# Delta heads' triangular inverses: the level of width 32 on packed 32x32 blocks, and two turns as products with the unit block

## The reference, cut to what matters

```
Gamma = jnp.exp(jnp.where(incl, G[..., :, None] - G[..., None, :], -jnp.inf))
kb = kc * bc[..., None]
A = jnp.where(strict, jnp.einsum('nbhcd,nbhsd->nbhcs', kb, kc) * Gamma, 0.0)
Tinv = lax.linalg.triangular_solve(eye + A, jnp.broadcast_to(eye, A.shape), left_side=True,
                                   lower=True, unit_diagonal=True)
u = jnp.einsum('nbhcs,nbhse->nbhce', Tinv, vc * bc[..., None])
w = jnp.einsum('nbhcs,nbhsd->nbhcd', Tinv, kb * jnp.exp(G)[..., None])
```

## Time and profile before

| | us |
|---|---|
| median of 3 runs | 2392.61 |
| lowest and highest run | 2390.42, 2393.23 |
| span of the profiled execution | 2388.0 |
| TensorE busy in it | 2303.5 (96%) |
| VectorE busy | 1345.3 (56%) |
| ScalarE busy | 580.2 (24%) |
| GpSimd busy | 185.4 (8%) |

### The profile page before, as it was taken

The page is one execution under the profiler, slowest core; times in us unless marked ns, Lnnn a source line. Parts: engine busy times, 40 slices in busy tenths (PEclk is TensorE's granted clock), DMA queues, the critical chain, the costliest instruction groups (busy, mean ns, idle before and its releaser), DMA issues.

```text
span 2388.0 us, 35106 instructions
## 1 busy us (share of the span) xinstructions
PE 2303.5 (96%) x13789; PEld 1951.4 (82%) x13789; DVE 1345.3 (56%) x2163; ACT 580.2 (24%) x1483; POOL 185.4 (8%) x252
## 2 busy tenths in 40 slices
PE   6999999999998999899999999999999999989998
PEld 3788889964546888788888999888899968668997
DVE  4377748564544777346776585677646521545521
ACT  3111111222222444441111113211111211442210
POOL 1100000001111333000000000000000000000000
PEclk7999999999999999999999999999999999999999
DMA  8555548532210000123555575355455523023562
GB/s 290 203 159 176 177 114 237 133 96 74 67 57 32 1 1 1 37 71 107 176 175 165 140 214 152 97 173 176 142 137 149 165 71 106 18 71 124 176 181 66
DMA packets 311468, 293.11 MB, mean 123 GB/s; under 512 B 6713, under 2 KB 292019, under 8 KB 311219
## 3 DMA queue, kind: packets, MB, share of 16 engines
q1 hardware_dynamic: 290611, 215.90, 30.5%
q0 software_dynamic: 20736, 75.51, 10.1%
HBM read 290.34 MB, written 1.05 MB: 122 GB/s over the span
## 4 chain that ended last, share of the span: by engine, by line
PE 89%; DVE 4%; ACT 3%; issue 1%; DMA 1%; SPq 0%; POOL 0%; DVEq 0%; POOLq 0%; ACTq 0%
PE bank L810 39%; PE bank L932 17%; PE bank L664 13%; PE bank L1010 3%; PE bank L774 2%; PE bank L1308 2%; PE bank L1130 2%; PE bank L1141 1%; PE bank L1069 1%; DMA mring<-in_w_mod 1%; PE bank L642 1%; DVE room L2374 1%; PE bank L1100 1%; PE bank L1151 1%; ACT hs L1726 1%
## 5 line engine op out<-in xcount | busy, mean ns | idle before, releaser
L810 PE MATMUL bank<-hs,ring 128*128 128x256 f32 (+1 forms) x2112 | 446.8, 356 | 5.6 <-ACT hs L1480 4.8
L810 PEld LDWEIGHTS bank<-hs,ring 128*128 128x128 f32 x2112 | 366.2, 192 | 54.6 <-issue 11.0
L932 PE MATMUL bank<-big,ring 128*128 128x128 f32 x2904 | 330.1, 275 | 0.0
L932 PEld LDWEIGHTS bank<-big,ring 128*128 128x128 f32 x2904 | 327.4, 192 | 0.2
L810 PE MATMUL bank<-room,big 128*128 128x256 f32 (+1 forms) x1408 | 296.1, 353 | 0.0
L810 PEld LDWEIGHTS bank<-room,big 128*128 128x128 f32 x1408 | 242.4, 191 | 26.6
L1928 DVE SCALAR_TENSOR_TENSOR mring<-mring,cond 128x1024 f32<-128x1024 f32 x196 | 240.4, 1279 | 9.9 <-DMA mring<-in_w_mod 9.9
L664 PE MATMUL bank<-hs,ring 128*128 128x512 f32 (+2 forms) x592 | 233.4, 548 | 0.0
L664 PEld LDWEIGHTS bank<-hs,ring 128*128 128x128 f32 (+1 forms) x592 | 109.8, 188 | 105.9 <-issue 102.2
L544 POOL DMA_DIRECT2D mring<-in_w_mod x144 | 76.2, 529 | 1074.0 <-DVE mring L1922 487.4
L810 PE MATMUL bank<-room,ring 128*128 128x256 f32 (+1 forms) x704 | 149.3, 355 | 2.5 <-ACT room L1516 1.8
(11 more groups left out here) (317 smaller groups left out, 3171.7 us busy)
## 6 DMA issues: line engine op xcount, KB each, us to landing
ring<-in_ffn_w_in SPq DMA_DIRECT2D x88, 1024.0 KB, 5.7
ring<-in_ffn_w_out SPq DMA_DIRECT2D x56, 1408.0 KB, 7.3
mring<-in_w_mod POOLq DMA_DIRECT2D x144, 512.0 KB, 4.1
ring<-in_gdn_w_in SPq DMA_DIRECT2D x16, 1024.0 KB, 5.7
ring<-in_diff_w_in SPq DMA_DIRECT2D x12, 1024.0 KB, 5.1
ring<-in_gdn_w_out SPq DMA_DIRECT2D x4, 1024.0 KB, 4.9
ring<-in_diff_w_out SPq DMA_DIRECT2D x4, 1024.0 KB, 4.9
cst<-in_consts SPq DMA_DIRECT2D x1, 1344.0 KB, 10.0
```

Of the source, the lines that this page charges most:

```text
L810: last = mm(bank[:, (g0 + b) % 4, 0:width], w[:, k, jj * P:(jj + 1) * P], rhs[:, k, 0:width], start=start and k == 0, stop=(k == KC // 2 - ...
L932: last = mm(bank[:, (go + b) % 4, 0:P], w[:, k, :], rhs[:, k, :], start=start and k == 0, stop=(k == FH - 1), skip_group_check=True)
```

## The change

At the level of width 32 (q = 2) only four 32x32 blocks of each chunk's matrix matter: for each pair `k` of quarters, `quarters(d, k)` names the quarter `r` whose rows change and the other, `o`. The change computes these alone.

- `level_p1` and `level_y` at width 32 are, for each direction and chunk, two products of 32x32 by 32x32 in place of one of 128x128, each into the rows of its quarter, at the 32 columns of the chunk (`packed_quarter`). Written products at each place: 16 for 8.
- `mask_p1` there is a copy of 128x128 for each direction in place of a multiplication of 128x512 by the mask.
- `update_y` there is two subtractions of 32 rows by 4x32 columns for each direction in place of one of 128x512.
- The turn after width 16 (q = 1) makes only the two 32x32 blocks that the next product reads, as products of the block of `yy` with the 32x32 unit block: 16 written products, two passes each, for 8 transpositions of one pass. `copy_t` puts them into a new tile `tq`, 128x128 for each direction, in place of 128x512.
- The turn after width 32 (q = 2) makes only the 64x64 block that the level of width 64 reads, as products with the 64x64 unit block: 8 written products for 8 transpositions. `copy_t` copies 64 rows by 4x64 columns.

Nothing else in the program is moved: the semaphores, the waits and the order of the steps stay. Between the steps of a full round stand full-size matmuls, so that each of the four places is a change of tile size on TensorE and one back.

```diff
@@ -329,6 +329,7 @@
         root_o = carve(NC)
         k_sum = carve(HEADS * NC)
         k_inv = carve(HEADS * NC)
+        tq = carve(2, P)
         LEFT = KC * 256
         below = [ring[:, 3, LEFT:LEFT + TOK], ring[:, 1, LEFT:LEFT + TOK]]
         rows_at = ring[:, 2, LEFT:LEFT + TOK]
@@ -378,6 +379,20 @@
 
         def packed_half(t):
             return slice(t * HALF, (t + 1) * HALF)
+
+        QUARTER = P // 4
+        quarter_rows = [slice(r * QUARTER, (r + 1) * QUARTER) for r in range(4)]
+
+        def quarter_of(t, r):
+
+            return slice(t * P + r * QUARTER, t * P + (r + 1) * QUARTER)
+
+        def packed_quarter(t):
+            return slice(t * QUARTER, (t + 1) * QUARTER)
+
+        def quarters(d, k):
+
+            return 2 * k + d, 2 * k + 1 - d
 
 
         def rounds(one_round):
@@ -1126,8 +1141,14 @@
                             else:
                                 of("t_copied", g, 2 * (n_lev - 1), 2 * (q - 1) + d + 1)
                             for t in range(NC):
-                                if LEVELS[q] < HALF:
+                                if LEVELS[q] < QUARTER:
                                     last = mm(bank[:, d, ch[t]], m2t[g % 2][:, d, ch[t]], tt_[:, d, ch[t]], start=True, stop=True)
+                                elif LEVELS[q] == QUARTER:
+                                    for k in range(2):
+                                        r, o = quarters(d, k)
+                                        last = mm(bank[quarter_rows[o], d, packed_quarter(t)],
+                                                  m2t[g % 2][quarter_rows[r], d, quarter_of(t, o)],
+                                                  tq[quarter_rows[r], d, packed_quarter(t)], start=True, stop=True)
                                 else:
                                     last = mm(bank[rows_of[1 - d], d, packed_half(t)], m2t[g % 2][rows_of[d], d, half_of(t, 1 - d)],
                                               tt_[rows_of[d], d, half_of(t, d)], start=True, stop=True)
@@ -1137,8 +1158,13 @@
                         for d in range(2):
                             of("p1_masked", g, 2 * n_lev, 2 * q + d + 1)
                             for t in range(NC):
-                                if LEVELS[q] < HALF:
+                                if LEVELS[q] < QUARTER:
                                     last = mm(bank[:, d, ch[t]], p1m[:, d, ch[t]], yy[g % 2][:, d, ch[t]], start=True, stop=True)
+                                elif LEVELS[q] == QUARTER:
+                                    for k in range(2):
+                                        r, o = quarters(d, k)
+                                        last = mm(bank[quarter_rows[r], d, packed_quarter(t)], p1m[quarter_rows[o], d, packed_quarter(t)],
+                                                  yy[g % 2][quarter_rows[o], d, quarter_of(t, o)], start=True, stop=True)
                                 else:
                                     last = mm(bank[rows_of[d], d, packed_half(t)], p1m[rows_of[1 - d], d, packed_half(t)],
                                               yy[g % 2][rows_of[1 - d], d, half_of(t, 1 - d)], start=True, stop=True)
@@ -1148,7 +1174,16 @@
                         for d in range(2):
                             of("y_updated", g, 2 * n_lev, 2 * q + d + 1)
                             for t in range(NC):
-                                last = turn(bank[:, d, ch[t]], yy[g % 2][:, d, ch[t]], ident)
+                                if q == 0:
+                                    last = turn(bank[:, d, ch[t]], yy[g % 2][:, d, ch[t]], ident)
+                                elif q == 1:
+                                    for k in range(2):
+                                        rows = quarter_rows[quarters(d, k)[0]]
+                                        last = mm(bank[rows, d, packed_quarter(t)], yy[g % 2][rows, d, quarter_of(t, quarters(d, k)[0])],
+                                                  ident[rows, rows], start=True, stop=True)
+                                else:
+                                    last = mm(bank[rows_of[d], d, packed_half(t)], yy[g % 2][rows_of[d], d, half_of(t, d)],
+                                              ident[rows_of[d], rows_of[d]], start=True, stop=True)
                             last.then_inc(S["t_turned"], 1)
 
                     def turn_k(g, n):
@@ -1625,7 +1660,14 @@
                     def copy_t(g, q):
                         for d in range(2):
                             of("t_turned", g, 2 * (n_lev - 1), 2 * q + d + 1)
-                            fn(tt_[:, d, :], bank[:, d, :], ACT.Copy).then_inc(S["t_copied"], 1)
+                            if q == 0:
+                                last = fn(tt_[:, d, :], bank[:, d, :], ACT.Copy)
+                            elif q == 1:
+                                last = fn(tq[:, d, :], bank[:, d, 0:P], ACT.Copy)
+                            else:
+                                last = fn(chunks(tt_[rows_of[d], d, :])[:, :, rows_of[d]],
+                                          bank[rows_of[d], d, 0:NC * HALF].rearrange("p (t c) -> p t c", t=NC), ACT.Copy)
+                            last.then_inc(S["t_copied"], 1)
 
                     def copy_k(g):
                         of("k_turned", g, 1, 1)
@@ -2400,9 +2442,11 @@
                     def mask_p1(g, q):
                         for d in range(2):
                             of("p1_done", g, 2 * n_lev, 2 * q + d + 1)
-                            if LEVELS[q] < HALF:
+                            if LEVELS[q] < QUARTER:
                                 last = v_.tensor_tensor(chunks(p1m[:, d, :]), chunks(bank[:, d, :]),
                                                         over_chunks(f"lev{d}_{LEVELS[q]}"), ALU.mult)
+                            elif LEVELS[q] == QUARTER:
+                                last = v_.tensor_copy(p1m[:, d, 0:P], bank[:, d, 0:P])
                             else:
                                 last = v_.tensor_copy(p1m[rows_of[1 - d], d, 0:NC * HALF], bank[rows_of[1 - d], d, 0:NC * HALF])
                             last.then_inc(S["p1_masked"], 1)
@@ -2410,8 +2454,14 @@
                     def update_y(g, q):
                         for d in range(2):
                             of("y_done", g, 2 * n_lev, 2 * q + d + 1)
-                            if LEVELS[q] < HALF:
+                            if LEVELS[q] < QUARTER:
                                 last = v_.tensor_tensor(yy[g % 2][:, d, :], yy[g % 2][:, d, :], bank[:, d, :], ALU.subtract)
+                            elif LEVELS[q] == QUARTER:
+                                for k in range(2):
+                                    r, o = quarters(d, k)
+                                    y = chunks(yy[g % 2][quarter_rows[r], d, :])[:, :, quarter_rows[o]]
+                                    last = v_.tensor_tensor(y, y, bank[quarter_rows[r], d, 0:P].rearrange("p (t c) -> p t c", t=NC),
+                                                            ALU.subtract)
                             else:
                                 y = chunks(yy[g % 2][rows_of[d], d, :])[:, :, rows_of[1 - d]]
                                 last = v_.tensor_tensor(y, y, bank[rows_of[d], d, 0:NC * HALF].rearrange("p (t c) -> p t c", t=NC),
```

## The result

| | before | after |
|---|---|---|
| median, us | 2391.52 (4 runs) | 2373.81 (4 runs) |
| lowest and highest | 2390.04, 2393.23 | 2371.42, 2374.60 |
| span of the profiled execution | 2388.0 | 2372.1 |

The ratio of after to before is 0.9922, with a 95% interval from 0.9910 to 0.9934: 18 us less, between 16 and 21. It falls beyond the rival of full overlap, priced at 2378. One execution of the kernel before, taken beside the traces e12 to e15, lasted 2453.64 us at a mean granted clock of 0.935, where all its others had 0.983 to 0.986; it enters no comparison.

The account below looks back on a forecast made before the run. TensorE up to the masked width-32 product, then VectorE's list, bound a full round in series. Gains of 4.9 (six full rounds), 1.8 (first) and 0.9 us (last), 7.6 together, plus 4.6 carried over, gave 2385.0 us, range 2377 to 2398.

Parts of the forecast that it names:

- the rival of full overlap: 32x32 segments: two tiles always work at once, p near 16 ns, 14.7 us less in all, 2378 us; chance 0.17.
- What bounds a full round: Full round: TensorE up to the masked width-32 product, then VectorE's list in series; gain is the reductions' earlier start, 0.82 us.
- the terms: Parts priced per round: VectorE's copies 0.29 us each, four subtractions 1.2; rounds give 4.9, 1.8 and 0.9 us, together 7.6.
- I take p = 29 ns: 32x32 segments on TensorE: each pass takes 29 ns, between bounds of 16 and 58.
- S: Length of a 32x32 segment of 32 passes on TensorE: 0.23 + 32p, 1.16 us.
- 0.29 was charged: Turn after width 16 in a full round: goes from 0.87 to 1.16 us, costing 0.29.
- The 4.6 us carried over from the span to the median: Whole kernel: median 2392.61 lies 4.6 us above the profiled span of 2388.0, added to 2380.4 to give 2385.0.
- the signs of being wrong that the prediction named: Profile after: full rounds staying at 31.2 us, 32-row subtractions taking 0.4 or more, or TensorE ending the round.
- That passes might cost 58 or 62 ns whatever their width: Slower rival in 32x32 segments: 58 ns a pass whatever its width, segment 2.09 us, +10.4 us, 2403 us; chance 0.14.
- the rule on one PSUM bank: New products: different row tiles cannot access one bank simultaneously, so p is 31.5 ns, some 1 us less gain in all.
- The turn after width 32: Full round: 0.87 us plus the wait becomes about 1.0, partly under the second subtraction; TensorE keeps pace, 0.82 gain survives.

Follow-up runs that it names:

- e12: The kernel before, unedited, profiled a second time: 2393.45 us in one run.
- e15: The changed kernel with both turns undone, profiled a second time: 2380.34 us in one run.
- e2: Changed kernel with VectorE's copy in place of the width-32 mask done twice per direction: full round 29.88 us for 29.49; 2387.05 us in one run.
- e3: Changed kernel with every pass of the second width-32 product issued twice: full round 29.48 us for 29.49; 2376.80 us in one run.
- e1: Changed kernel issuing all passes of a direction's first pair of quarters before its second pair's: full round 30.02 us for 29.49; 2377.85 us in one run.
- e11: Changed kernel with every pass of the second width-32 product issued eight times, 256 in a row: 2433.69 us in one run.
- e4: Changed kernel with the turn after width 16 again 128x128 transpositions and 128x512 copies: full round 29.80 us for 29.49; 2382.26 us in one run.
- e5: Changed kernel with both turns again 128x128 transpositions and 128x512 copies: median 2383.02 us, ratio to the kernel before 0.9961.
- e6: Kernel before with only the turn after width 32 made of 64x64 products with its smaller copy: full round 31.42 us for 31.26; 2394.07 us in one run.
- e7: Changed kernel with the copies replacing masks at widths 32 and 64 on ScalarE and the first reduction earlier: median 2371.16 us, ratio to the kernel before 0.9919.
- e9: Changed kernel with mask copies on ScalarE, first reduction earlier and TensorE's matmul of the blocks earlier in quarter 3: 2364.84 us, ratio to kernel before 0.9886.

## Why the prediction was wrong

**What bounds a full round** was right. VectorE's list from the reductions on sets it (e2, e3), its length did not change (11.76 for 11.70 us), and the copies took 0.29 us and the four subtractions 1.19, as the terms had it.

**The failed step is "I take p = 29 ns".** The rows gave the pieces: a tile takes a pass every 32 ns by the extrapolation from 111 and 58, and two tiles can start passes within a few ns. The trace after confirms both. Passes of L1182 that had started since 805.60 (L1182 alone, columns as in the earlier trace rows):

```profile
805.60:805.78 0.18, 0.06 (x4) 0.07 (x6) 1.00 0.00 0
...
805.60:805.84 0.24, 0.12 (x8) 0.12 (x9) 1.00 0.00 0
```

Four have started by 805.78 and eight by 805.84: four in 60 ns, two tiles with a pass each in about 30. So each of two tiles keeps its own pitch; e1 shows one tile alone at 31 to 32 ns. What I then took was the mean rate of two tiles of 64x64, 58 / 2 = 29 ns, because it lies near the 31.5 of one tile of 32x32. That gives the alternation of the new passes nothing. Against full overlap I held that the segment of 64x64 had taken 1.00 us. But there all passes of a direction go to one tile and overlap only where the second direction's begin; in the new segments consecutive passes alternate between two tiles. e1 sends eight in a row to one tile again and gets 0.82 us for 0.53. e3 and e11 give 16 ns a pass for two tiles, which I had as the extreme. Even this extreme was too high: the second direction uses two more tiles and starts before the first is done. Between 805.92 and 805.97 eight passes start where two tiles alone would start three:

```profile
805.60:805.92 0.32, 0.20 (x14) 0.20 (x18) 1.00 0.00 0
805.60:805.97 0.37, 0.25 (x22) 0.26 (x24) 1.00 0.00 0
```

So the 32 passes of a segment start within 0.41 us, 13 ns each. With the 0.10 us of entering ahead of it the segment is 0.63 us where S was 1.16; some 0.10 more shows on the full-size passes behind it.

**The price in the sum.** The turn, the first product and the copies took 1.8 us off a full round ahead of the reductions instead of 0.82; the turn saves 0.34 (0.87 to 0.53) where 0.29 was charged. Six full rounds give 10.6 us for 4.9, the first 2.9 for 1.8, the last 2.2 for 0.9: 15.7 for 7.6. That is 8 of the 11 us missed.

**The other 3 us** (2385.0 less 8.1 is 2376.9, and 2373.8 was measured) are two things. The median of three runs that the forecast started from, 2392.61, lies 1.1 above the median of four, 2391.52: luck of the draw. And the medians differ by 17.7 us where the terms give 15.7. Of these 2.0, 1.4 are the stretch at half clock near 766 that the change takes away, which I had not in the sum at all; 0.6 is within the scatter. The 4.6 us carried over from the span to the median were no cost of their own: a run's time lies 1.7 us above its own span (2373.77 against 2372.1), and the other 2.9 say only that the profiled execution was a quick one against that median (the three spans of the kernel before are 2388.0, 2391.8 and 2385.3).

**The rivals.** Full overlap, at 0.17, was the case that came: its 1.65 us a full round, 2.6 for the first and 2.2 for the last stand beside 1.77, 2.9 and 2.2. It should have been the likeliest, since the code alternates tiles. Its price of 2378 was 4 us too slow, by the same 3 us as above and by 15.7 for 14.7 in the terms. None of the signs of being wrong that the prediction named came: full rounds fell to 29.5, the four subtractions took 1.19 and VectorE still ends the round. It named none for the fast side. That passes might cost 58 or 62 ns whatever their width is refuted for this length of run: 32 passes start in 0.41 to 0.42 us in every segment of 32x32 of the trace after, and e11 shows 216 in a row. The sentence of the Trainium skill, "TensorE: Matmul & The Clock Gate", section "Wait — 56ns, not 53.3ns?", on 62 ns a MATMUL with hardware decode off does not describe what this trace shows; whether hardware decode was on here is on no record. Of the rule on one PSUM bank (the Trainium skill, "TensorEngine Tiling (Array Packing)", "Restrictions and Gotchas") this can be said: the two tiles of a direction have different rows of the array and write the same bank in different partitions, and the counts above show both at the pitch that e1 shows for one tile alone, 31 to 32 ns; no cost of sharing the bank appears.

**The turn after width 32** was priced near nothing in full rounds, and in the changed kernel it is (0.04 us against, e4 and e5). Alone in the kernel before it costs 0.16 (e6), because TensorE's place in front of VectorE's solve is nearer than my sum had it.

## What to carry to other kernels

Before pricing small matmuls, write down for each pass in its order which tile of the array it uses (rows from the operands' partitions, columns from the output's). Consecutive passes on one tile cost the pitch of a tile, consecutive passes on two tiles half of it, and a segment measured with the one order is no price for the other (e1: 0.82 us for 0.53). Where two engines' lists are in series, look for what can move into the waits of either: here that gave more than half as much again as the change (e7 and e9). And read the clock beside the work before a difference of medians is explained by work alone: two turns with 2.4 us of work moved the median by 9.

## What the runs showed of the hardware

- One tile of TensorE took a 32-bit pass of 64x64 every 58 ns (L1132 in the earlier trace rows) and one of 32x32 every 32 ns (e1). Two tiles in alternation gave 15 to 16 ns a pass over 216 passes (e11); four in part 13 ns over 32 (L1182 after).
- Between two segments of small tiles four full-size passes stood for 0.64 us (806.25 to 806.89) where they take 0.45 among their like: some 0.19 us for leaving the one and entering the other.
- Each of eight runs of 256 small passes was stopped for 0.79 to 1.59 us with no cause in the trace, and the granted clock fell to half within 3.2 us of the start of that stop, for 3.4 or 17.1 us (e11).
- The granted clock fell for 3.4 us at the same places in every trace of a kernel (near 765 in three of three before, in none of three after; three places in two of two with the turns undone), while at the start of the first round, after 2.9 us of idle TensorE, it fell for anything from 0 to 10.2 us.
- A wait of some 0.75 us of TensorE for VectorE ahead of L1185 preceded stretches at half clock in three of five full rounds (e2); with 0.44 us there were none.
